# Two-layer MLA + RWKV-7 encoder trunk: an RWKV block's front made one round ahead, its triangle products moved into the level's gaps, and two output-projection tiles loaded ahead of the feed-forward weights

## The reference

```
w_t = exp(-exp(-softplus(-(w0 + tanh(xw) @ w2)) - 0.5))     a_t = sigmoid(a0 + xa @ a2)
k_d = k * (1 + (a - 1) * k_a)                               kk = k * k_k, normalised per head
S_t = S_{t-1} * w_t + (S_{t-1} @ -kk_t) (kk_t * a_t)^T + v_t k_d^T ;   y_t = S_t r_t
y   = groupnorm(y_forward + y_backward) * gn_g + gn_b
out = (y + (sum(r * (k_f + k_b) / 2 * r_k)) * v) * g,       g = sigmoid(xg) @ g2
```

## Time and profile before

| what | value |
|---|---|
| timed runs | 1922.97, 1926.53, 1933.13 us; median 1926.53 |
| profiled execution | 1921.93 us, its span 1920.0 us |
| PE busy | 1686.8 us (88%), mean granted clock 0.902 |
| DVE, ACT, POOL busy | 1011.2, 731.6, 289.0 us |
| chain that ended last | PE 58%, issue 25%, DVE 7%, ACT 5%, POOL 3%, DMA 1% |
| first instruction of the levels, layer 0 (L551) | 321.2, 376.0, 436.1, 487.7 us |
| output projection, layer 0 | about 529 to 588 us |

### The profile page before, as it was taken

How to read it: one execution, slowest core, us unless ns; L and a number is a source line. 1 busy time by engine, 2 the same in 40 slices (tenths; PEclk the granted TensorE clock), 3 DMA queues, 4 the chain that set the end, 5 groups by cost and what they waited for, 6 DMA issues and landing times.

```text
span 1920.0 us, 27840 instructions
## 1 busy us (share of the span) xinstructions
PE 1686.8 (88%) x11192; PEld 1254.9 (65%) x11192; DVE 1011.2 (53%) x1533; ACT 731.6 (38%) x1193; POOL 289.0 (15%) x124
## 2 busy tenths in 40 slices
PE   2997865988998999999989978588889899999997
PEld 0784434766766888877757834276666688887785
DVE  6654557767416677664443244676653354445333
ACT  3434244556533322322233343455555332233222
POOL 1341000000021222211224400000000222222221
PEclk8998985788899999999989989677689999999999
DMA  7344110000032545543303310000002122222231
GB/s 285 137 159 145 58 61 1 2 2 2 2 121 95 201 175 186 203 146 144 123 11 122 97 55 0 1 2 2 2 2 78 55 88 91 106 87 89 86 103 72
DMA packets 34652, 162.98 MB, mean 85 GB/s; under 512 B 3840, under 2 KB 4096, under 8 KB 25856
## 3 DMA queue, kind: packets, MB, share of 16 engines
q1 hardware_dynamic: 34560, 161.65, 23.8%
HBM read 159.54 MB, written 2.10 MB: 84 GB/s over the span
## 4 chain that ended last, share of the span: by engine, by line
PE 58%; issue 25%; DVE 7%; ACT 5%; POOL 3%; DMA 1%; POOLq 0%; DVEq 0%; ACTq 0%; SPq 0%
PE bank L497 7%; PE bank L499 7%; PE bank L498 7%; PE bank_pair L497 3%; PE bank_pair L499 3%; PE bank_pair L498 3%; PE bank_pair L588 2%; POOL work_parts L1873 2%; PE bank L815 2%; PE bank L816 2%; PE bank L793 1%; PE bank L517 1%; PE bank L557 1%; PE bank L567 1%; PE bank L600 1%
## 5 line engine op out<-in xcount | busy, mean ns | idle before, releaser
L497 PE MATMUL bank<-work_parts,y_mix_parts 128*128 128x512 f32 x792 | 315.2, 398 | 21.3 <-DVE work_parts L1645 10.3
L499 PE MATMUL bank<-work_parts 128*128 128x512 f32 x792 | 314.5, 397 | 0.0
L1658 DVE TENSOR_TENSOR work_parts<-work,y_mix_parts 128x1024 fp32r<-128x1024 f32 x66 | 169.2, 2564 | 258.1 <-ACT y_mix_parts L941 258.1
L1868 POOL TENSOR_TENSOR proj_weights_parts<-proj_weights,proj_weights_hi 128x1024 fp32r<-128x1024 f32 x54 | 130.1, 2418 | 990.4 <-ACT proj_weights_hi L937 914.9
L1873 POOL TENSOR_TENSOR work_parts<-work,y_mix_parts 128x1024 fp32r<-128x1024 f32 x66 | 158.7, 2405 | 608.4 <-ACT y_mix_parts L941 608.4
L941 ACT ACTIVATE y_mix_parts<-work 128x1024 fp32r<-128x1024 f32 x132 | 133.0, 1054 | 263.9 <-DMA work<-mlp_dram 254.2
L498 PE MATMUL bank<-work_parts,y_mix_parts 128*128 128x512 f32 x528 | 208.7, 395 | 0.0
L497 PEld LDWEIGHTS bank<-work_parts,y_mix_parts 128*128 128x128 f32 x792 | 150.5, 190 | 59.2 <-issue 25.0
L499 PEld LDWEIGHTS bank<-work_parts 128*128 128x128 f32 x792 | 150.1, 190 | 35.5
L497 PE MATMUL bank<-work_parts,proj_weights_hi 128*128 128x512 f32 x272 | 111.8, 411 | 26.3 <-DVE work_parts L1645 23.8
L498 PEld LDWEIGHTS bank<-work_parts,y_mix_parts 128*128 128x128 f32 x528 | 99.8, 189 | 24.1
(11 more groups left out here) (262 smaller groups left out, 3116.3 us busy)
## 6 DMA issues: line engine op xcount, KB each, us to landing
work<-mlp_dram SPq DMA_DIRECT2D x66, 1024.0 KB, 4.8
work<-ada_dram SPq DMA_DIRECT2D x64, 512.0 KB, 4.7
proj_weights<-tiles_dram SPq DMA_DIRECT2D x57, 512.0 KB, 3.6
x_res<-ada_dram SPq DMA_DIRECT2D x24, 512.0 KB, 4.7
x_res<-x_dram SPq DMA_DIRECT2D x2, 2048.0 KB, 10.4
mixer_inputs<-ada_dram SPq DMA_DIRECT2D x8, 512.0 KB, 17.3
work<-mlaw_dram SPq DMA_DIRECT2D x4, 640.0 KB, 4.3
out_dram<-x_res SPq DMA_DIRECT2D x8, 256.0 KB, 2.2
```

The costliest lines, as they stand in the source:

```text
L497: mm(out, w_hi, x_hi, start=start, stop=False)
L499: return mm(out, w_lo, x_hi, start=False, stop=stop)
L1658: TTT(MW_L[q][:, 1], MW_IN[q][:, 1], plain(MW_H[q][:, 1]), ALU.subtract).then_inc(msp_v.sem, msp_v.one("l1"))
L1868: pool.tensor_tensor(ring_l[s], ring[s], plain(ring_h[s]), ALU.subtract).then_inc(spl_q.sem, spl_q.one(f"t{s}"))
```

## The change

Two buffers are rearranged so that a block's front can be made while the block before is still in its inverse: `CW` shares `PI`, and `PP` lies in slot 0 of the ring of rounded weights, unused during RWKV. The LoRA products write banks 5 and 6 instead of 1 and 2. A round now makes the front of nxt + 1: W behind scan step 4, A behind step 6, the decay sums within the last step of DVE's inverse, exponentials and factors on ACT before the level, queries, removals, keys and bonus on DVE beside the level. The level holds the triangle products of the next block, one after T and one after Z. So DVE's inverse begins in step 0. Bonus, centre, variance and gate move, the tail's norm goes ahead of the next level, and ACT copies the centred values to free bank 5. For the first block of a layer front and triangles run ahead of the first round. SP loads tiles 22 and 23 ahead of the first two feed-forward weights, and adaLN's pair behind three more tiles.

```diff
-        LW, AA, CW, PP, PI = [[WORK[:, 17952 + 1024 * i + 512 * d:18464 + 1024 * i + 512 * d] for d in range(2)] for i in range(5)]
+        LW, AA, PI = [[WORK[:, o + 512 * d:o + 512 * d + 512] for d in range(2)] for o in (17952, 18976, 22048)]
+        CW, PP = PI, [RING_P[:, 512 * d:512 * d + 512] for d in range(2)]
...
@@ SP
                 sp.wait_ge(tl_v.sem, tl_v.at("gt", l * RB + RB - 1))
+                for t in range(NPROJ, NPROJ + 2):
+                    load_tile(l, t)
                 for q in range(2):
                     sp.dma_start(MW_IN[q], mlp[l * NMLP + q]).then_inc(mlp_in[q], 16)
+                for t in range(NPROJ + 2, NTILE - 3):
+                    load_tile(l, t)
                 if l + 1 < DEPTH:
                     load_ada(0)
-                for t in range(NPROJ, NTILE - 3):
-                    load_tile(l, t)
...
@@ PE, rwkv_triangle and rwkv_level
+                if d == 0:
+                    pe.wait_ge(ear_a.sem, ear_a.at("A1", it))
...
+                if early:
+                    rwkv_triangle(it + 1, 0)
                 scan_values(it, 0)
                 scan_tokens(it, b, 1)
...
+                if early:
+                    rwkv_triangle(it + 1, 1)
...
@@ PE, rwkv_round
-                    if build and s in (0, 1):
-                        rwkv_triangle(new, s)
-                    if build and s == 3:
+                    if trail and s == 0:
+                        if build:
+                            pe.wait_ge(tri_a.sem, tri_a.at("B10", new))
+                        tail_centre(old)
+                    if build and s == 0:
                         rwkv_bonus(new)
...
+                    if early and s == 4:
+                        if trail:
+                            pe.wait_ge(tl_a.sem, tl_a.at("ln", old))
+                        else:
+                            pe.wait_ge(bon_v.sem, bon_v.at("bon", new))
+                        rwkv_early(new + 1, nxt + 1, 0)
+                    if early and s == 6:
+                        rwkv_early(new + 1, nxt + 1, 1)
                 if scan:
                     own(sc_p, last, "Y")
-                if early:
-                    rwkv_early(new + 1, nxt + 1, scan)
                 if build:
                     scan_gram(new, 0)
                     scan_tokens(new, nxt, 0)
+                    if trail:
+                        if early:
+                            pe.wait_ge(ear_a.sem, ear_a.at("A1", new + 1))
+                        tail_gate(old, cur - 1)
                     rwkv_level(new, nxt, scan, early)
...
@@ ACT, rwkv_round (s is the scan step)
+                    if build and s == 0:
+                        triangle(new, 1)
...
+                    if trail and s == 1:
+                        tail_square(old)
+                    if trail and s == 3:
+                        tail_log(old)
+                    if early and s == 5:
+                        early_decay(new + 1, nxt + 1)
+                    if trail and s == (6 if build else 4):
                         tail_scale(old)
+                    if early and s == 6:
+                        early_shift(new + 1)
+                    if early and s == 7:
+                        early_rate(new + 1, nxt + 1)
...
                 if early:
+                    factors(new + 1, nxt + 1)
                 if build:
                     scan_ring(new, 0)
+                    level(new, early)
...
@@ DVE, rwkv_round
+                        if s == 0:
                             inverse_in(new)
                             inverse_half(new)
+                        if s == 1:
+                            bonus_end(new, nxt)
+                            inverse_8(new, 1, 5)
+                        if s == 2:
+                            inverse_8(new, 5, 8)
+                            inverse_16_first(new)
...
+                        if s == 6:
+                            inverse_32_second(new)
+                        if s == 7:
+                            if early:
+                                for d in D2:
+                                    decay_sum(new + 1, d)
+                            inverse_32_end(new)
+                            inverse_out(new)
...
+                if build:
+                    scan_ring(new, 0)
+                    if trail:
                         tail_norm(old, cur - 1)
+                    if early:
+                        if scan:
+                            dve.wait_ge(sc_p.sem, sc_p.at("Y", it))
+                        queries(new + 1, nxt + 1, 0)
+                        removals(new + 1, nxt + 1, 0)
+                    for q in range(2):
+                        diagonal(new, q)
+                    if early:
+                        queries(new + 1, nxt + 1, 1)
+                        removals(new + 1, nxt + 1, 1)
+                    scan_ring(new, 1)
+                    if early:
+                        front_sums(new + 1, nxt + 1)
```

More of the change, by code:

```diff
@@ L136, in trunk @@
         RING, RING_R = two_names("proj_weights", 3 * KD * P)
[L137 removed]
+        RING_P, RING_H = two_names("proj_weights_hi", 3 * KD * P)
         SQ = sb("squares", 2 * SEQ)
@@ L502, in own, with rwkv_early @@
                 ins.then_inc(s.sem, s.one(name))
[L504 to L515, removed]
-                        rows = slice(64 * d, 64 * d + 64)
-                        own(ear_p, mm(PS[1 + d][:, :], l_rw[rows, b, i, :], mix(x)[rows, :], start=True, stop=True), f"{n}{d}")
+            def rwkv_early(it, b, i):
+                n, x = (("W", XW), ("A", XA))[i]
+                for d in D2:
+                    if i == 1:
+                        pe.wait_ge(ear_a.sem, ear_a.at(f"W{d}", it))
+                    rows = slice(64 * d, 64 * d + 64)
+                    own(ear_p, mm(PS[5 + d][:, :], l_rw[rows, b, i, :], mix(x)[rows, :], start=True, stop=True), f"{n}{d}")
             def rwkv_triangle(it, d):
                 pe.wait_ge(pre_v.sem, pre_v.at(f"b{d}", it))
+                if d == 0:
+                    pe.wait_ge(ear_a.sem, ear_a.at("A1", it))
                 if d == 0 and it % RB >= 3:
@@ L839, in _ @@
                 pe.wait_ge(on_a.sem, on_a.at("rs", l))
-                rwkv_early(l * RB, 0, False)
+                pe.wait_ge(lora_in, (l + 1) * 16)
+                for i in range(2):
+                    rwkv_early(l * RB, 0, i)
+                for d in D2:
+                    rwkv_triangle(l * RB, d)
                 for cur in range(-1, RB):
@@ L1092, in tail_square @@
                 own(tl_a, F(YQ, PS[5][:, :], ACT.Square), "sq")
+                own(tl_a, F(mix(R0 + it % RB), PS[5][:, :], ACT.Identity), "cp")
             def y_head(l, k):
@@ L1111, in rwkv_round @@
                 scan, build, trail, early = cur >= 0, nxt < RB, cur > 0, nxt + 1 < RB
-                if build and not scan:
-                    for d in D2:
-                        grown(new, d)
-                    for d in D2:
-                        shrunk(new, d)
                 for s in range(NCH):
@@ L1121, in rwkv_round @@
                             scan_ring(it, s + 1)
+                    if build and s == 0:
+                        triangle(new, 1)
+                    if scan:
                         scan_solve(it, s)
-                    if build and s == 0:
-                        factor(new, nxt, 0)
-                        factor(new, nxt, 1)
-                    if build and s in (0, 1):
-                        triangle(new, s)
-                    if build and scan and s == 4:
+                    if build and s == 1:
+                        inverse_rows(new)
@@ L1153, in rwkv_round @@
+                    if early and s == 7:
+                        early_rate(new + 1, nxt + 1)
+                    if not build and s in (0, 2, 5):
+                        if s == 5:
+                            act.wait_ge(tl_v.sem, tl_v.at("gt", old - 1))
+                        first = (0, 2, 5).index(s) * 2
+                        y_head(l, first)
+                        y_head(l, first + 1)
                 if scan:
@@ L1625, in rwkv_round @@
                         if s == 5:
[L1626 removed]
+                            inverse_32_mid(new)
                         if s == 6:
[L1628 to L1635 removed]
```

171 lines of the change are left out of this document (65 added, 106 removed).

## The result

| what | before | after |
|---|---|---|
| median of the timed runs | 1924.75 us (4 runs) | 1870.44 us (4 runs, 1868.72 to 1877.9) |
| ratio, 95% interval | | 0.9724, 0.9675 to 0.9774 |
| profiled execution, its span | 1921.93, 1920.0 us | 1868.72, 1866.8 us |
| PE busy, mean granted clock | 1686.8 us, 0.902 | 1645.5 us, 0.926 |
| levels R0 to R3, layer 0 | 321.2, 376.0, 436.1, 487.7 us | 319.5, 366.7, 417.05, 465.9 us |

What follows compares the result with a forecast made beforehand. No engine was full; PE was nearest, losing time to order and its low clock. RWKV terms of -10.5 us a layer (-21.0) and -8.8 for the output projection gave -29.8: 1926.5 to 1896.7 us, range 1882 to 1917.

Steps and rivals of the forecast that it cites:

- Level: Opening part of a round, up to the first solve: two triangle products come in, net +1.9 us, +3.5 in the third.
- Scan: First solve to update of step 6: triangles and waits go out; -3.3, -3.4 and -5.7 us in the first three rounds.
- keeps its parts: 0: Last round of a layer: its parts stay as before, so no change in time, 0 us.
- the meetings on DVE: Scan steps: state products falling behind pieces of DVE's inverse, charged 0.5 us a round, +1.5 a layer.
- the preamble: Ahead of a layer's first round: inverse starts 1.4 us earlier but ends 2.33 later by the decay scans, +0.9 us.
- A rival on the clock: RWKV rounds: low clock lasts longer, slower than before from 2.6 steps' delay, 1941 us with four; chance 0.05.
- that rule: ACT table loads: the Trainium skill's 1380 ns drain beside each load; estimated 8 us, leaving 1905; the forecast sided against it.
- End: Update of step 6 to next level: DVE chain as floor, 8.8 us in the first two rounds, -3.2 and -4.6.
- Output projection: Tile 22 loaded ahead of feed-forward weights: -6.0 us in layer 0, -2.8 in layer 1, -8.8 together.
- DVE is busy: Rival, scan steps: DVE becomes the bound, waits of up to 0.8 us a step, 24 us in all, about 1919; chance 0.12.
- Half the gain: Rival, levels: second triangle in the open and b0 1 us late, six levels cost 15 us more, 1912; chance 0.17.
- The projection idle: Rival, output projection: its part does nothing because tile 22 still lands late, 1905 us; chance 0.06.

Runs made afterwards that it cites:

- e9: The changed kernel, unchanged, executed and profiled a second time: 1875.93 us, ratio 0.9757.
- e3: The changed kernel with both triangle products behind Z, out of the level's middle: 1893.26 us, ratio 0.9839.
- e12: The changed kernel with dummy 128x128 by 128x512 products: seven or four ahead of levels, one behind gram, one behind T, none in the triangle-less level: 1867.02 us.
- e4: The changed kernel with dummy 128x128 by 128x512 products, three ahead of each level and five ahead of the first: 1869.61 us, ratio 0.9706.
- e1: The kernel before with only SP's new load order for the output projection: 1915.29 us, ratio 0.9956.
- e10: The changed kernel with SP's load order of before, the projection's part undone: 1885.31 us, ratio 0.9798.
- e2: The kernel before with small dummy products on 64x32 tiles behind T and ahead of Z in six levels: 2006.28 us, ratio 1.042.
- e5: The changed kernel with both triangles behind Z and one dummy 128x128 by 128x512 product in the first triangle's place: 1888.45 us, ratio 0.9832.
- e6: The kernel before with one dummy 128x128 by 128x512 product between T and the values in six levels: 1932.55 us, ratio 1.0027.
- e8: The changed kernel with one dummy 128x128 by 128x512 product behind each level's gram, and one behind T in the triangle-less level: 1889.01 us, ratio 0.9831.

## Why the prediction was wrong, point by point

| layer 0, us | forecast | after | e9 | e3 | e12 |
|---|---|---|---|---|---|
| R0 | 50.2 | 47.2 | 50.1 | 50.8 | 45.4 |
| R1 | 54.0 | 50.4 | 50.5 | 53.9 | 48.7 |
| R2 | 49.4 | 48.9 | 48.9 | 51.1 | 44.6 |
| R3 on | 94.4 | 91.7 | 94.6 | 94.6 | 94.5 |
| level of R0, R1, R2 | 15, 15, 14.3 | 13.5, 13.8, 14.8 | 15.3, 13.8, 14.7 | 16.6 each | 11.7 each |
| first solve to update of step 6 | 26.5, 30.1, 28.6 | 25.0, 28.0, 27.1 | 26.2, 28.0, 27.2 | 25.5, 28.6, 27.5 | 25.0, 28.0, 26.5 |

*The step that failed* is the one under "Level" and "Scan" that carried over from before where the clock rises, "some 20 us into the round": it priced every product of the level at its low-clock duration, and step 0 at 4.4 us. After has the rise at +9.4 in R0 and +10.0 in R1. In layer 0 the surplus over the forecast is 3.0 us in R0, 3.6 in R1, 0.5 in R2 and 2.7 in R3, where "keeps its parts: 0" assumed the old clock too. The clearest evidence is the kernel after itself: where its rise is late, R0 takes 49.8 to 50.1 us and R3 on 94.6, against the 50.2 and 94.4 of the forecast; where it is early, 47.2 and 91.7. In R1, e3's late rise gives 53.9 us for the 54.0 of the forecast.

*How much of the surplus is the clock.* The gain was 24.5 us over the forecast. An early rise for a late one is worth 2.9 us in R0 and 2.9 in R3 (rows of the same kernel), and some 2.8 in R1 (e3's 53.9 less 50.4, less 0.7 by which e3's late R0 is longer than after's). That is an estimate of 17 us for both layers. e3's 23 us hold more than the rise: its wait between the triangles, and the difference between the first runs of after and e9. Of the rest, 3.0 us are the meetings on DVE, which were charged and did not come, and 1.6 the preamble; 2.7 are left in the sums of the levels and scans.

*The range.* A rival on the clock was there, but only with the low clock lasting longer; its mirror had no place, neither among the rivals nor among the signs of being wrong, and so the lower end of the range, 1882, was wrong as well.

*Not all of that is the change's own.* Of the 24.5 us, R0 and R3 (some 3 us each in a layer) fall out differently from one execution to the next. The median of e9 is 5.5 us above that of the first set of runs, and its profiled execution is 5.1 above the first (1873.8 against 1868.72): 5.8 more in one R0 and one R3, 2.0 more ahead of the first level, 2.8 less between the layers. What stays is R1, eight times of eight. That the new order also makes the early rise in R0 more frequent is not shown: three of eight against none of two in before and none of two in e3.

*Level.* +1.9 was the net of two triangles with the second hidden in the 1.6 us wait. In after that wait is 0.60 us and the second triangle takes 1.10 in front of it: hidden, as said. With the late rise the level takes 15.3 (e9), near my 15. A triangle at the low clock takes 1.93 us; the 1.76 of the earlier trace rows was read from one during which the clock rose. In e3 the second triangle waits 1.28 us for ACT's copies and then stands in the open: 16.6 us, 1.6 over my 15. b0 was never late in a level of after or e9; in e4, where the level of R2 begins at the high clock, PE waits 1.44 us for it, as the forecast said of the high clock.

*Scan.* The removal of the triangles and waits was right in size; the charges were too high. ACT holds PE up 0.77 us in step 1 of R1 (forecast 0.9) and 0.29 in step 5 (0.6). The meetings on DVE, 1.5 us a layer beside these sums, did not come. And "step 6 up to its update is 2.4" was too much: the steps before it were counted from solve to solve, and from the solve of step 6 at 421.05 to the end of its update at 422.75 are 1.7. In R0 of after it is 1.56:

```profile
356.48 0.45 PE L641 MATMUL bank<-rstd,work 64*64 64x64 f32 x8
...
357.59 0.45 PE L651 MATMUL bank<-work 128*64 128x64 f32 x8 [0.27 <-ACT work L1097]
```

That is why e3's scans, with the late rise, are still 1.0 to 1.5 us under the forecast, and make up for part of its longer levels. ACT in step 1 of R1, kernel after:

```profile
387.80 1.28 ACT L941 ACT_TABLE_LOAD   x1
389.10 0.20 ACT L941 ACTIVATE spare<-constants 128x1 f32<-128x1 f32 x1
389.31 0.60 ACT L1110 ACTIVATE squares<-bank 128x512 f32<-128x512 f32 x1
```

with the solve of step 2, which waits for it on PE:

```profile
390.62 0.45 PE L641 MATMUL bank<-rstd,work 64*64 64x64 f32 x8 [0.77 <-ACT rstd L1090]
```

The load takes 1.28 us and the next instruction starts at its end: the moved load brought no drain of 1.4 us, as the forecast's weighing of that rule had it.

*End.* 8.8 us were forecast for R0 and R1, 8.6 came; PE waits 3.80 us for the transposition, 3 were said. In R2 the DVE chain was to stay at 6.4: it is 6.9 in after and 6.4 in e12. *Preamble:* +0.9 was forecast; front to level is 38.8 us for 39.0 in layer 0, 39.95 for 39.56 in layer 1, about 0. *Output projection:* the gaps behind tile 21 gave back 6.0 and 2.8 us, as forecast; by the times it is 8.5 (e1) and 9.4 (e10).

*The rivals.* DVE is busy 37.5 to 38.1 us in R0 to R2, and in R0 to R3 of layer 0 PE waits for a state product twice, 0.16 us each: out. Half the gain: out, levels are shorter than forecast. The projection idle: out by e1. The clock was the decisive one, with its sign reversed.

## What to carry to other kernels

Where a stretch of many small products runs at the low clock, the place of the clock's rise is a term of the sum like any other, with both signs: where it falls in the kernel before tells only what the old order of work got. Ask of a moved product not only what it takes, but whether it stands in the low stretch and may end it; price the stretch at both levels and put both in the range. And profile a kernel twice before a few us of one round are put down to the change: here the same code had two values for R0, 47.2 and 50.1 us.

## What the runs showed of the hardware that was not expected

- PE busy without a gap does not by itself bring the high clock: 24 us, nearly all of 64x32 and 32x32 tiles, stayed at 0.50 (e2). The Trainium skill ("TensorE: Matmul & The Clock Gate", Part 1, What's actually happening) has the clock follow how busy PE is; these rows do not agree where the products are that small.
- Dummy 128x128 by 128x512 products in the idle time before a level and twice within it kept 1.00 through six levels but for 3 us (e12); three to five ahead of it alone did not (e4). One within it went with the early rise in R1 and R2 of e5, but not in R0 of e5, in R0 and R1 of e6 or in five levels of six in e8.
- The same code rises at +9.4 or at +19.3 us (R0 of after and of e9). The same section also says that where the rise falls varies from run to run, by 500 ns either way; these rows agree that it varies, and not with that size, since it is 10 us here.
- What exactly decides between the two in R0, and why R1 of the kernel after is always early, stays open. That the clock is still high some 4 us ahead of R1's level in after and e5, and not in before and e6, fits, but e3 and e8 have that too and were late: it is not shown.
